# One multiply by the inverse row sums moved behind two more score steps in the later-half attention units

## The reference

```python
s = q @ k.T / 8 - slope * distance + log(count)     # -1e30 where no pattern has the key
p = exp(s - m);  l = sum(p);  o = (p @ v) / l
y_b = o * silu(b_gate)
merged = g_a * (y_a @ w_proj_a) + g_b * (y_b @ w_proj_b)
```

## Time and profile before

| | |
|---|---|
| median of three runs | 2457.62 us |
| the profiled execution's own time | 2457.08 us |
| its span, first to last instruction | 2455.4 us |
| PE busy | 2395.0 us (98%) |
| PE weight loads busy | 1978.2 us (81%) |
| VectorE busy | 1234.9 us (50%) |
| ScalarE busy | 801.7 us (33%) |
| POOL busy | 636.0 us (26%) |
[...]
| attention units | about 1570 to 2162 us of the span |

### The profile page before, as it was taken

The page is one execution under the profiler, slowest core; times in us unless marked ns, Lnnn a source line. Parts: engine busy times, 40 slices in busy tenths (PEclk is TensorE's granted clock), DMA queues, the critical chain, the costliest instruction groups (busy, mean ns, idle before and its releaser), DMA issues.

```text
span 2455.4 us, 29786 instructions
## 1 busy us (share of the span) xinstructions
PE 2395.0 (98%) x11260; PEld 1978.2 (81%) x11260; DVE 1234.9 (50%) x1649; ACT 801.7 (33%) x1166; POOL 636.0 (26%) x326
## 2 busy tenths in 40 slices
PE   8999999999999999999999999999999999999997
PEld 6888788878888888888888888887787877878886
DVE  4444754764444433263221112578777777753534
ACT  4421223242323321143211111355455555541221
POOL 2221222265555422222121121212111111121221
PEclk9999999999999999999999999999999999999998
DMA  3111222232222332222222233332332332344223
GB/s 131 44 44 35 95 77 102 70 146 86 83 89 78 120 137 86 69 77 78 103 86 86 86 111 120 103 108 79 105 120 77 103 102 78 111 163 137 100 89 111
DMA packets 66148, 234.63 MB, mean 96 GB/s; under 512 B 7936, under 2 KB 8080, under 8 KB 66064
## 3 DMA queue, kind: packets, MB, share of 16 engines
q1 hardware_dynamic: 51376, 179.98, 22.4%
q10 hardware_dynamic: 14688, 53.48, 5.4%
HBM read 175.76 MB, written 57.67 MB: 95 GB/s over the span
## 4 chain that ended last, share of the span: by engine, by line
PE 95%; DVE 3%; issue 1%; DMA 1%; ACT 0%; DVEq 0%; SPq 0%; ACTq 0%
PE dense L685 23%; PE dense L687 23%; PE dense L686 23%; PE dense L836 5%; PE dense L838 5%; PE dense L837 5%; PE aux L963 2%; PE aux L947 2%; PE aux L948 1%; PE aux L976 1%; PE aux L975 1%; PE aux L910 1%; DVE att_p_lo L1945 1%; PE aux L715 0%; PE aux L790 0%
## 5 line engine op out<-in xcount | busy, mean ns | idle before, releaser
L685 PE MATMUL dense<-x_hi,w_hi 128*128 128x512 f32 x2032 | 822.3, 405 | 15.0 <-DVE x_lo L1499 13.6
L687 PE MATMUL dense<-x_hi,w_lo 128*128 128x512 f32 x2032 | 795.1, 391 | 0.0
L686 PE MATMUL dense<-x_lo,w_hi 128*128 128x512 f32 x2032 | 794.8, 391 | 0.0
L590 POOL TENSOR_TENSOR w_lo<-w_raw,w_hi 128x1024 fp32r<-128x1024 f32 x159 | 387.3, 2436 | 1417.6 <-ACT w_hi L1035 1413.0
L1035 ACT CAST w_hi<-w_raw 128x1024 fp32r<-128x1024 f32 x158 | 166.0, 1051 | 888.8 <-PE dense L687 868.5
L685 PEld LDWEIGHTS dense<-x_hi,w_hi 128*128 128x128 f32 x2032 | 383.9, 189 | 87.5 <-issue 16.8
L687 PEld LDWEIGHTS dense<-x_hi,w_lo 128*128 128x128 f32 x2032 | 382.9, 188 | 82.3
L686 PEld LDWEIGHTS dense<-x_lo,w_hi 128*128 128x128 f32 x2032 | 384.4, 189 | 69.3 <-issue 2.2
L1540 DVE TENSOR_TENSOR work<-dense,rstd 128x1024 f32<-128x1024 f32 x97 | 118.5, 1222 | 406.1 <-PE dense L687 397.7
L625 POOL TENSOR_TENSOR w_lo<-w_sums,w_hi 128x512 fp32r<-128x512 f32 x76 | 118.2, 1563 | 125.2 <-ACT w_hi L1187 125.2
L1368 ACT CAST att_p_hi<-aux 128x512 fp32r<-128x512 f32 x192 | 92.1, 480 | 146.9 <-PE aux L963 146.5
(11 more groups left out here) (235 smaller groups left out, 3280.6 us busy)
## 6 DMA issues: line engine op xcount, KB each, us to landing
w_raw<-weights SPq DMA_DIRECT2D x179, 512.0 KB, 3.8
kept_qkv<-work ACTq DMA_DIRECT2D x24, 512.0 KB, 2.6
kept_m<-work ACTq DMA_DIRECT2D x22, 512.0 KB, 2.6
work<-kept_m SPq DMA_DIRECT2D x22, 512.0 KB, 3.5
w_raw_b<-weights SPq DMA_DIRECT2D x18, 512.0 KB, 4.4
residual<-xT SPq DMA_DIRECT2D x16, 512.0 KB, 6.9
kept_x<-residual ACTq DMA_DIRECT2D x16, 512.0 KB, 2.7
att_q<-kept_qkv SPq DMA_DIRECT2D x32, 256.0 KB, 3.8
```

Of the source, the lines that this page charges most:

```text
L590: pool.tensor_tensor(WL[:, u.slot], WR[:, u.slot], WH[:, u.slot].bitcast(f32), ALU.subtract).then_inc(w_lo, 1)
L685: pe.matmul(dst, WH[:, u.slot, k], hi, start=(k == 0), stop=False)
L686: pe.matmul(dst, WH[:, u.slot, k], lo, start=False, stop=False)
L687: last = pe.matmul(dst, WL[:, u.slot, k], hi, start=False, stop=(k == nk - 1))
```

## The change

In the odd string of DVE_STEPS, n0 (block 0's reciprocal and multiply) moves from behind z to behind r4, so l0, r3 and r4 now come before it; n1 moves from before l1 to behind r5. Nothing is added or removed, and PE, ScalarE, POOL and the DMA queues have the same instructions in the same order.

```diff
 DVE_STEPS = [
     "O l0 k l1 z l2 r0 l3 r1 n0 l4 r2 n1 l5 r3 n2 l6 m n3 l7",
-    "v0 r0 v1 O r1 r2 z n0 l0 r3 r4 n1 l1 r5 m r6 r7 l2 n2 b l3 n3 q",
+    "v0 r0 v1 O r1 r2 z l0 r3 r4 n0 l1 r5 n1 m r6 r7 l2 n2 b l3 n3 q",
 ]
```

## The result

The changed kernel takes 2433.45 us in the median of four runs (2432.42 to 2436.65) against 2457.64 us of the kernel before (2453.29 to 2459.62): the ratio is 0.9907, 95% interval 0.9891 to 0.9923, 24.2 us less. The forecast was 2433.9 us, with a range of 2427 to 2442. The profiled execution itself took 2433.82 us, 23.3 less than the one before, at a mean granted clock of 0.995 of full speed against 0.994.

A forecast was written before the change was run, and what follows sets the result against it. PE, 98% busy, was taken to be bound by s5 stalls from n0 held by POOL; 8 x 1.40 + 7 x 1.33 + 1.03 + 1.7 = 23.2 us off 2457.08 gives 2433.9 us, range 2427 to 2442.

The forecast's parts named there:

- What bounds: PE's s5 waits for r3 in 16 late units, 24.9 us, because POOL's w_lo holds n0 on VectorE.
- The stall goes: PE at s5 in late units: wait gone, worth 2.06 us in first-head units, 1.40 in second-head ones.
- The shadow at nothing: l0 and r3, now beside POOL's w_lo on VectorE, are not lengthened; costed at nothing.
- The price, 0.73 us in first-head units: n1 in front of m delays m, POOL's att_mixed multiply, n2, b, l3 and PE's o3 by 0.73 us.
- the other signs of being wrong: Among them: t0 of the next unit waiting for n3, or k sliding under w_lo and being held.
- Second-head units: No m or att_mixed multiply there; VectorE's slack at r7 lets the whole 1.40 us return, bounds 0.67 to 1.40.
- The full block as rival: A held multiply needs its whole duration after POOL: n2's hold 0.69, not 0.49 us; 2435.5 us, chance 0.08.
- The clock term: Stretches at 1.2 GHz behind two s5 stalls may vanish: 1.7 us saved, middle of 0 and 3.4.
- the upper bound: Both clock falls behind s5 stalls go, each worth 1.7 us of PE work: 3.4 us.

The follow-up runs named there:

- run 5: Kernel before, its order kept, with n0's multiply in late units cut to 128 of 640 columns: 2451.54 us, ratio 0.9984.
- run 6: Kernel before, its order kept, with POOL making only 256 of 1024 columns of w_lo in late units: 2432.33 us, ratio 0.9905.
- run 7: Kernel before with n0 moved only behind l0, still in front of r3, n1 in its old place: 2444.61 us, ratio 0.9956.
- Run 2: Changed kernel with n1 put back in front of l1, n0 staying behind r4: 2427.71 us, ratio 0.9882.
- run 8: Changed kernel with n1 moved behind m: 2431.31 us, ratio 0.9906.
- run 4: Changed kernel with n1 back in front of l1 and b moved behind n3: 2427.68 us, ratio 0.9887.
- run 1: Changed kernel measured again, unedited: 2431.83 us, ratio 0.9906 against the kernel before.
- run 3: Changed kernel with b moved from in front of l3 to behind n3: 2430.96 us, ratio 0.9901.

## Why the prediction was right

*What bounds.* n0 held by POOL, its own length irrelevant: shown from three sides, by a shorter n0 that stayed long (run 5), a shorter w_lo that freed it (run 6) and an n0 moved too little (run 7).

*The stall goes.* s5 at its place on PE in all sixteen units, none waiting: 2.06 and 1.40 us as costed. From s5 of a second-head unit to s5 of the next first-head one PE took 1815.76 - 1777.87 = 37.89 us and takes 1807.16 - 1771.44 = 35.72, 2.17 less: the 2.06 and 0.11 more, on which below.

*The shadow at nothing.* The l steps stayed at 687 ns. They and the r steps have one input in PSUM, and neither kind lengthened: r3, now in w_lo's shadow, takes 0.47 or 0.48 us in all sixteen units, 0.47 before.

*The price, 0.73 us in first-head units.* To the digit on the chain (t1 to o3, 8.51 against 7.78). Run 2 shows that it was the place of n1 and nothing else. PE waits 0.64 us at o3 where I expected 0.6 to 0.8. Of the other signs of being wrong none came: no t0 waits for n3, and k keeps its 1.22 or 1.23 us.

*Second-head units.* The full stall, no wait at o3: VectorE still waits 0.28 us for PE at r7 (0.43 before), so the slack was there:

```profile
1776.00 0.75 DVE L1926 CUSTOM_DVE_ANT_0 att_p_late<-aux,att_bias,softmax_stats 128x512 f32<-128x512 f32 x1 [0.28 <-PE aux L948]
```

*The full block as rival.* It falls. A multiply freed by POOL ended 0.08 us (128 columns, run 5), 0.34 (640), 0.41 (768, run 8: 1589.65 + 2.78 against 1589.62 + 2.40) and 0.49 us (896) behind POOL's end, each some 0.2 us less than it lasts unheld: 0.29 (the early block of run 5), 0.55 and 0.62 (n0 and n1 of the changed kernel) and 0.69 (n2 in run 8, 687 ns in the mean of 16). Run 8 shows the wait in either direction: n1 took 2.78 us where POOL had started 0.03 us before it, POOL 2.82 us where n1 had started 0.06 us before it. That a held instruction owes its whole duration afterwards was the rival's assumption, and the rows show 0.2 us less. Whether the multiply has done these 0.2 us by then, or POOL's record ends that much later than its hold, no run tells.

*Where it was off by a little.* The stage gained 24.9 us, the sum said 23.2. One term was missing: a unit without a stall also saves at the restart. s5 to t1 took 1741.76 - 1740.83 = 0.93 us behind a stall and takes 1735.89 - 1735.08 = 0.81 without. Over the sixteen units it was 0.91 to 0.94, the two with a fall of the clock apart, and is 0.81 or 0.82: 0.11 x 16 = 1.8 us. It lies in the first matmul of s5. Behind a stall that matmul and its weight load both start at 1740.83, and the next matmul follows 0.29 us later; without one the load starts at 1734.91, the matmul at 1735.08 and the next 0.18 later, so there the load lies under the matmul ahead of it. In run 6 a wait of the load alone (0.27 us at 1770.36) is enough to give 0.92.

The clock term, 1.7 us, was the middle of two bounds, with no reason for the middle; that it came out near is luck. Its 1.2 GHz is an estimate for the bottom of a fall, with a column taken for a clock: there the traces give 0.50 of full speed (1666 to 1669 us of the profile before), and 128x512 matmuls start 0.43 us apart, not 0.23, which is 512 / 0.43 = 1.2 columns per ns. Both falls went, and each had cost about 1 us, not the 1.7 that the upper bound took. From s5 of a first-head late unit to s5 of the next late unit PE took 1853.94 - 1815.76 = 38.18 us with a fall and 1777.87 - 1740.83 = 37.04 without. Over the three traces of before it is 37.99 to 38.18 against 37.02 to 37.40, and in the last pair 37.93 against 36.61 and 36.65. So the two that went are worth about 2 us.

With both, 21.5 + 1.8 + 2 = 25.3 us, 0.4 more than measured. That stretch became some 37.1 - 36.4 = 0.7 us shorter where no fall was in it, and 1.40 + 0.11 - 0.73 = 0.78 was costed; what takes the difference no run shows. The whole time fell by less, 24.2 us in the medians and 23.3 in the profiled pair: outside the stage the changed kernel's profiled execution took 2432.1 - 554.2 = 1877.9 us against 2455.4 - 579.1 = 1876.3, and falls of the clock come and go there.

*Was it the best order?* No. n0 behind r4 is all that the gain needs; n1's move costs 5 us. Run 2 is the better kernel, 2427.7 us, and run 4, with one move more, is level with it.

## What to carry to other kernels

When one instruction of a form takes several times what its neighbours take (here 2252 ns for n0 against 621 for the longer n1), look for what POOL runs beside it and compare the two ends. An end that sticks to POOL's end whatever the start is a hold: n0 started 0.12, 0.80 and 1.21 us behind POOL and ended 0.34 to 0.36 us behind it each time. What stands behind it on VectorE pays, and l0, once out from behind it, gave 0.6 us a unit back (run 7). Move the held instruction behind POOL's end, not just later, and move nothing else with it: each neighbour that comes along must have a gap of its own to lie in, as n1 had 0.80 us in front of l1 (run 2). Two such instructions should not be placed to start together, for who is first was decided by 0.03 to 0.06 us in run 8, and n1 took 2.78 us where it lost.

## What was not expected of the hardware

- A held multiply owed some 0.2 us less than its duration when POOL's record ends: it ends 0.08, 0.34, 0.41 or 0.49 us behind POOL for 128, 640, 768 or 896 columns, where unheld it lasts 0.29, 0.55, 0.62 or 0.69. One that started 0.2 us before POOL's end (n0 in run 1) lost nothing.
- The hold worked both ways, decided by a few hundredths of a microsecond: n1 took 2.78 us instead of 0.62 beside a POOL multiply that started 0.03 us before it, POOL's multiply took 2.82 us instead of 2.41 behind an n1 that started 0.06 us earlier (run 8), and w_lo 2.68 us behind k, which reads two SBUF operands (run 3).
- The granted clock fell to 0.50 of full speed right behind five of the 21 waits of 1.91 us, and behind none of the waits of 1.65 us and less nor the one of 2.01 us, in twelve traces.
